# A V table split at column 1024, and every second dense block multiplied in three passes

## The reference

```
def peer_ffn(h, w_query, sub_keys, expert_u, expert_v):      # h: 256 tokens x 2048
    qc = (xc @ w_query).reshape(C, 8, 2, 128)                # 8 heads, two half keys each
    s = einsum('chpd,hpnd->chpn', qc, sub_keys)              # 128 keys per half
    top_s, top_i = top_k(s, 16)
    cand_s = top_s[:, :, 0, :, None] + top_s[:, :, 1, None, :]
    best_s, best_pos = top_k(cand_s over 16 * 16, 16)        # 16 experts of 128 * 128
    g = softmax(best_s)
    u, vv = expert_u[expert_idx], expert_v[expert_idx]       # rows of 2048 floats
    act = gelu(einsum('chkd,cd->chk', u, xc))
    return einsum('chk,chkd->cd', g * act, vv)
```

## Time and profile before

| | us |
|---|---|
| median of three runs | 1690.18 |
| lowest, highest | 1689.35, 1695.68 |
| the profiled execution | 1694.34 |
| its span, first to last instruction | 1692.5 |
| TensorE busy in the span | 1234.9 (73%) |
| VectorE busy | 1298.5 (77%) |
| GpSimd busy | 842.8 (50%) |
| ScalarE busy | 460.9 (27%) |
| moved by DMA | 575.81 MB, 340 GB/s on average |

### The profile page before, as it was taken

How to read it: one execution, slowest core, us unless ns; L and a number is a source line. 1 busy time by engine, 2 the same in 40 slices (tenths; PEclk the granted TensorE clock), 3 DMA queues, 4 the chain that set the end, 5 groups by cost and what they waited for, 6 DMA issues and landing times.

```text
span 1692.5 us, 14464 instructions
## 1 busy us (share of the span) xinstructions
PE 1234.9 (73%) x4812; PEld 839.8 (50%) x4812; DVE 1298.5 (77%) x1802; ACT 460.9 (27%) x1023; POOL 842.8 (50%) x546
## 2 busy tenths in 40 slices
PE   9999999999995554001344544454699999999993
PEld 7888887778984343000122322332365555555551
DVE  5554666466699999999999999999796665666667
ACT  5333443554200100000135565552381000000000
POOL 1000010000174888877888888888565443444444
PEclk9999999999997778555666676666699999999997
DMA  8886546348799999999999999999899999999998
GB/s 237 223 207 196 169 143 213 99 148 278 260 410 415 422 411 396 385 371 362 395 382 407 403 413 387 398 401 422 335 313 380 410 409 411 410 410 409 410 409 347
DMA packets 150230, 575.81 MB, mean 340 GB/s; under 512 B 15586, under 2 KB 28596, under 8 KB 117268
## 3 DMA queue, kind: packets, MB, share of 16 engines
q0 software_dynamic: 74384, 421.30, 62.6%
q1 hardware_dynamic: 75460, 152.82, 26.9%
q10 hardware_dynamic: 320, 0.86, 0.1%
HBM read 572.57 MB, written 2.36 MB: 340 GB/s over the span
## 4 chain that ended last, share of the span: by engine, by line
PE 30%; DVE 28%; DMA 24%; POOL 12%; issue 4%; ACT 2%; DVEq 0%; ACTq 0%; POOLq 0%
DMA v_rows<-in_peer_expert_v,pick_row 21%; DVE big L1549 10%; DVE more_rows L1549 8%; PE ps L1692 6%; PE ps L1694 6%; PE ps L1693 6%; POOL big L691 5%; PE ps L2095 4%; POOL more_rows L691 3%; DVE big L1597 3%; POOL v_rows L671 3%; DMA more_rows<-in_peer_expert_u,pick_row 2%; PE ps L2118 1%; DMA big<-in_peer_expert_u,pick_row 1%; DVE big L1574 1%
## 5 line engine op out<-in xcount | busy, mean ns | idle before, releaser
L671 POOL DMA_INDIRECT v_rows<-in_peer_expert_v,pick_row x256 | 307.8, 1202 | 271.7 <-DVE big L1597 234.9
L1597 DVE SCALAR_TENSOR_TENSOR big<-v_rows,pick_w,big 128x1152 f32<-128x1152 f32 x203 | 287.6, 1417 | 151.7 <-DMA v_rows<-in_peer_expert_v,pick_row 149.7
L2095 PE MATMUL ps<-v_rows,diag 128*128 128x512 f32 (+1 forms) x312 | 182.9, 746 | 269.5 <-DMA v_rows<-in_peer_expert_v,pick_row 169.8
L1549 DVE CUSTOM_DVE_ANT_0 big<-big 128x2048 f32<-128x2048 f32 x150 | 340.1, 2283 | 12.9 <-DMA big<-in_peer_expert_u,pick_row 12.5
L691 POOL DMA_INDIRECT big<-in_peer_expert_u,pick_row x150 | 288.8, 1925 | 65.6 <-issue 43.2
L2095 PEld LDWEIGHTS ps<-v_rows,diag 128*128 128x128 f32 x312 | 83.3, 285 | 368.2 <-issue 194.8
L691 POOL DMA_INDIRECT more_rows<-in_peer_expert_u,pick_row x106 | 222.7, 2101 | 75.3 <-issue 28.3
L1030 DVE TENSOR_TENSOR split_lo<-raw,split_hi 128x1024 fp32r<-128x1024 f32 x119 | 145.8, 1225 | 143.7 <-ACT split_hi L719 118.1
L1549 DVE CUSTOM_DVE_ANT_0 more_rows<-more_rows,big 128x2048 f32<-128x2048 f32 x106 | 240.8, 2284 | 11.0 <-DMA more_rows<-in_peer_expert_u,pick_row 11.0
L2127 PE MATMUL ps<-big,dense 128*128 128x512 f32 (+1 forms) x512 | 213.5, 539 | 0.3 <-DMA big<-in_peer_expert_v 0.3
L2127 PE MATMUL ps<-big 128*128 128x512 f32 (+1 forms) x512 | 213.4, 539 | 0.0
(11 more groups left out here) (281 smaller groups left out, 1495.2 us busy)
## 6 DMA issues: line engine op xcount, KB each, us to landing
big<-in_peer_expert_v SPq DMA_DIRECT2D x128, 448.0 KB, 6.8
raw<-in_w_in SPq DMA_DIRECT2D x88, 512.0 KB, 3.7
raw<-in_w_out SPq DMA_DIRECT2D x32, 512.0 KB, 5.1
big<-in_peer_w_query SPq DMA_DIRECT2D x16, 512.0 KB, 6.5
raw<-in_peer_w_query SPq DMA_DIRECT2D x8, 512.0 KB, 7.6
spare<-in_peer_w_query SPq DMA_DIRECT2D x8, 512.0 KB, 8.3
v_rows<-in_peer_expert_v,pick_row POOLq DMA_INDIRECT x256, 14.2
big<-in_peer_expert_u,pick_row POOLq DMA_INDIRECT x150, 9.1
```

What stands on the lines that cost most here:

```text
L671: pool.indirect_dma_start(v_row(k), None, v_table, bass.IndirectOffsetOnAxis(pick_row[:, k:k + 1], 0)).then_inc(v_gathered[v_place(k)], 16)
L1549: dve.tensor_tensor_reduce(row, row, XN[:, place_of(m // TOPK)[0], :], 1.0, 0.0, ALU.mult, ALU.add, pick_dot[:, m:m + 1]).then_inc(dotted, 1)
L1597: dve.scalar_tensor_tensor(out=v, in0=row, scalar=pick_w[:, k:k + 1], in1=v, op0=ALU.mult, op1=ALU.add).then_inc(added, 1)
L2095: ins = pe.matmul(psf[:, c:c + w], diag[:, j % DIAGS, :], row[:, c:c + w], start=k == 0, stop=j == pe_adds(PICKS) - 1)
```

## The change

- V_ROW goes from 1152 to 1024: a gathered V row set has 128 x 1024 floats, an add on VectorE is 1024 wide, and a dense block has 1024 columns where it had 896.
- The V buffer now holds 5 places in place of 7, since three places of 1024 columns are taken for high parts (`dense_hi`). The places in use beside the dots are 4 where they were 3.
- The U ring is narrow from gather 90 on (108 before), V gathers begin at the dot 99 (115 before), and 40 V picks are added by TensorE beside the dots (36 before). Behind the change-over (still 37 picks) 179 adds are left for VectorE, 183 before.
- Blocks 5, 7, ... 127 (62 of them) are "split blocks". ScalarE copies the block to float32r, and the two 128 x 128 weight blocks as well; VectorE subtracts to get the low parts, in place; TensorE makes three products in the place of one in full float32. The high weights are put where the weights of block a - 4 were.
- VectorE's low parts are put among its adds by `split_after`: those of block a about two blocks ahead of where an even spread of 179 adds over 128 blocks would have it. ScalarE stores the first tile's rows in the midst of its list, behind block 63.

The diff, cut to its core:

```diff
@@ -131,14 +131,14 @@
 RING = 8
 EARLY, EARLY_ROWS = 6, 12
 OLD_HT = 4
-U_WIDE = 108
+U_WIDE = 90
 NARROW = (2, 3, 0, 1, 6, 7)
 WEIGHED = 2
 
-V_ROW = 1152
+V_ROW = 1024
 V_DENSE = D - V_ROW
-V_FROM, V_BESIDE = 112, 36
-V_FIRST_PLACES, V_PLACES = 3, 7
+V_FROM, V_BESIDE = 96, 40
+V_FIRST_PLACES, V_PLACES = 4, 5
 DIAGS = 4
 
 TILE_PICKS = NH * TOPK
@@ -152,6 +152,15 @@
 V_AFTER = V_BESIDE + len(SEAM)
 TURN_BANK = 5
 DENSE_AT = (4 * 512, 6 * 512)
+HI_PLACES, HI_BEHIND = 3, 4
+SPLIT_BLOCKS = [a for a in range(HI_BEHIND, NKEYS) if a % 2]
+SPLIT_AHEAD = 2
+OUT_0_AT = 63
+
+
+def split_after(n):
+
+    return [a for a in SPLIT_BLOCKS if max(0, a - SPLIT_AHEAD) * (PICKS - V_AFTER) // NKEYS == n]
 
 
 def u_place(m):
@@ -384,6 +393,11 @@
         dense_w = (dense0, dense1)
         dense_rows = part(DENSE_PLACES * V_DENSE).rearrange("p (s n) -> p s n", s=DENSE_PLACES)
         assert A_XN <= at_big[0] - DENSE_PLACES * V_DENSE and at_big[0] <= A_X1T
+        at_rows = at_big[0] - DENSE_PLACES * V_DENSE
+        dense_lo = nc.alloc_sbuf_tensor_at("dense_lo", [P, DENSE_PLACES, V_DENSE], F32R, offset=at_sbuf["big"] + 4 * at_rows)
+        split_w = [nc.alloc_sbuf_tensor_at(f"split_w{t}", [P, NKEYS, P], F32R, offset=at_sbuf["big"] + 4 * (A_PROJ if t else A_X1T)) for t in range(TT)]
+        dense_hi = nc.alloc_sbuf_tensor_at("dense_hi", [P, HI_PLACES, V_DENSE], F32R, offset=at_sbuf["ht"])
+        assert HI_PLACES * V_DENSE + V_PLACES * V_ROW <= OLD_HT * D
         hot0 = ring_rest.rearrange("p (s j n) -> p s j n", s=2, j=GROUP_TOKENS)
         hot_at = at_big[0] - (DENSE_PLACES - DENSE_EARLY) * V_DENSE
         hot1 = part(SEAM_HOT * 2 * GROUP_TOKENS * P, hot_at).rearrange("p (i s j n) -> p i s j n", i=SEAM_HOT, s=2, j=GROUP_TOKENS)
@@ -412,6 +426,7 @@
         query_loaded = {n: sem(f"query_loaded_{n}") for n in
                         [k + str(i) for k in ("ahead", "raw", "spare", "ring") for i in range(RAW)] + ["pqt1", "pqt2", "pqt3", "rest0"]}
         query_used = sem("query_used")
+        dense_high, dense_split = sem("dense_high"), sem("dense_split")
 
         def query_name(n):
 
@@ -999,9 +1014,18 @@
                 if ("pe", i) in SEAM_V:
                     pick_diag(SEAM_V["pe", i])
             group_out(1, GROUPS - 1)
-            act.wait_ge(sem("out_ready"), 1)
-            act.wait_ge(added, dve_adds(TILE_PICKS))
-            act.dma_start(out_rows[:, 0, 0:V_ROW], X[:, 0, 0:V_ROW]).then_inc(out_stored, 16)
+            act.wait_ge(group_moved, TT * GROUPS)
+            for r, a in enumerate(SPLIT_BLOCKS):
+                act.wait_ge(dense_loaded[a % DENSE_PLACES], 16 * (a // DENSE_PLACES + 1))
+                act.wait_ge(dense_used, a - HI_BEHIND + 1)
+                act.activation(dense_hi[:, r % HI_PLACES, :], dense_rows[:, a % DENSE_PLACES, :], ACT.Copy).then_inc(dense_high, 1)
+                for t in range(TT):
+                    ins = act.activation(split_w[t][:, a - HI_BEHIND, :], dense_w[t][:, a, :], ACT.Copy)
+                ins.then_inc(dense_high, 1)
+                if a == OUT_0_AT:
+                    act.wait_ge(sem("out_ready"), 1)
+                    act.wait_ge(added, dve_adds(TILE_PICKS))
+                    act.dma_start(out_rows[:, 0, 0:V_ROW], X[:, 0, 0:V_ROW]).then_inc(out_stored, 16)
             act.wait_ge(dense_used, NKEYS)
             v = slice(V_ROW, V_ROW + CHUNK)
             act.activation(X[:, 1, v], ps[:, 6, :], ACT.Copy).then_inc(sem("dense_copied"), 1)
@@ -1654,7 +1678,20 @@
                 hot_pair(i)
                 if ("dve", i) in SEAM_V:
                     v_add(SEAM_V["dve", i])
+            def split_low(a):
+
+                r = SPLIT_BLOCKS.index(a)
+                dve.wait_ge(dense_high, 2 * r + 1)
+                dve.tensor_tensor(dense_lo[:, a % DENSE_PLACES, :], dense_rows[:, a % DENSE_PLACES, :],
+                                  dense_hi[:, r % HI_PLACES, :].bitcast(F32), ALU.subtract).then_inc(dense_split, 1)
+                dve.wait_ge(dense_high, 2 * r + 2)
+                for t in range(TT):
+                    ins = dve.tensor_tensor(split_w[t][:, a, :], dense_w[t][:, a, :], split_w[t][:, a - HI_BEHIND, :].bitcast(F32), ALU.subtract)
+                ins.then_inc(dense_split, 1)
+
             for k in range(V_AFTER, PICKS):
+                for a in split_after(k - V_AFTER):
+                    split_low(a)
                 if k == V_AFTER + V_PLACES:
                     tile_out(dve_adds(k))
                 v_add(k)
@@ -2119,6 +2156,19 @@
 
             def dense(a):
 
+                if a in SPLIT_BLOCKS:
+                    r = SPLIT_BLOCKS.index(a)
+                    pe.wait_ge(dense_split, 2 * r + 2)
+                    hi, low = dense_hi[:, r % HI_PLACES, :], dense_lo[:, a % DENSE_PLACES, :]
+                    for t in range(TT):
+                        w_hi, w_low = split_w[t][:, a - HI_BEHIND, :], split_w[t][:, a, :]
+                        for w, row in ((w_hi, hi), (w_hi, low), (w_low, hi)):
+                            for c in range(0, V_DENSE, CHUNK):
+                                o = DENSE_AT[t] + c
+                                last = a == NKEYS - 1 and w is w_low
+                                ins = pe.matmul(psf[:, o:o + CHUNK], w, row[:, c:c + CHUNK], start=False, stop=last, skip_group_check=True)
+                    ins.then_inc(dense_used, 1)
+                    return
                 pe.wait_ge(dense_loaded[a % DENSE_PLACES], 16 * (a // DENSE_PLACES + 1))
                 row = dense_rows[:, a % DENSE_PLACES, :]
                 for t in range(TT):
```

## The result

The changed kernel took 1717.57 us as the median of four runs (1713.71 to 1718.29), against 1690.36 us before (with one run more than the three of the table above). The ratio is 1.0155 with a 95% interval of 1.0137 to 1.0173: 1.6% slower, where 0.4% faster was forecast, and above the range of 1672 to 1712. It is within half a microsecond of the time that rival 1 gave for a load chain that sets the pace (1718), but that agreement of the numbers is partly luck, as the part on why the prediction was wrong shows.

A forecast was written before the change was run, and what follows sets the result against it. TensorE and DMA were both full in the dense stage, the bound passing to TensorE. TensorE + 10.4, stalls + 6, end - 16.6, U stage - 4, change-over - 2 made 6.2 us less: median 1684.0 us, range 1672 to 1712.

The forecast's parts named there:

- rival 1: Dense stage: the load chain makes TensorE wait for split blocks' low parts; 1718 us at 7.8 us landing; chance 17%.
- The bound: Dense stage: TensorE and DMA both full; bound passes to TensorE at 395.7 us, DMA needing 381.
- TensorE's own term, + 10.4: Dense stage: without waits TensorE ends 10.4 us later; widening costs 55 us, three passes give back 45.
- The stalls: Dense stage: TensorE waits for split blocks' loads, 0.1 us a pair, 6 us in all.
- the bounds 0 and 40: Dense stage: lowest and highest total of TensorE's stalls in us, for load landings from 3.6 to 7.8 us.
- The rule of the Trainium skill: Dense stage: DMA engines alternate between gather and load queues, so loads land as before, 6.8 us; stalls 9 us.
- a point of 6.5: Dense stage: landing time in us up to which nothing stalls; beyond it 30 us for each microsecond.
- The gather ring: Dense stage: five V places are just enough; a gather may take 9.4 us, landing 8 to 10 instead of 14.4.
- Rival 2: Dense stage: five gather places starve VectorE if a gather needs 10.2 us; 29 us more, 1707; chance 11%.
- The U stage and the change-over: Before the dense stage: earlier, smaller V gathers save 4 us in the U stage; narrower adds save 2 in the change-over.
- The end: Behind TensorE's last product: the span ends 9.5 us later instead of 26.1, so 16.6 us come back.
- two of the signs: Wrong if TensorE waits over 20 us for low parts, split products are not near 0.226, or U stage ends later.

The follow-up runs named there:

- The kernel with the fifth place: The changed kernel with a fifth place for dense blocks, taken from one of three places of high row parts: 1693.40 us, ratio 1.0011.
- a sixth place: The changed kernel with six places for gathered V rows instead of five, and two for high row parts instead of three: 1708.45 us, ratio 1.0119.

## Why the prediction was wrong, step by step

**The bound.** Right that TensorE and DMA are both full, that TensorE's own work rises a little, and that the end comes back. TensorE's own term, + 10.4, was right within 1 to 3 us. The kernel without split blocks took 442.6 us from first product to TensorE's end, forecast 441.4. The changed kernel's 426.3 us less 61 x 0.47 of stalls, which come next, are 397.6, against 395.7 and about 1.1 for the last drain. The kernel with the fifth place took 402.9, of which 3 are by its period still waits.

**The stalls: the term that failed.** "I take 6.7, near the 6.6 to 6.8 of the stage ... That is 0.1 us a pair, 6 us in all; between the bounds 0 and 40." The mechanism stood there, with its place and its point of decision; its size was 6.63 - 6.16 = 0.47 us a pair, 29 us by the periods, and 24 by the medians with and without the fifth place. Two things made it so, in about equal parts.

The chain was longer, 10.18 us from the end of block a - 4 to TensorE's start on block a, where I had 9.8. The load is the part that was off: 7.14 us from its issue to ScalarE's start and not 6.7. VectorE's low part then came 1.26 us behind ScalarE and not 1.10, since VectorE was at times late out of an add, and the rest was 0.2 shorter than I had it. I had read the median of the landings, 6.8, where a loop goes by the mean: the odd blocks' was 7.00 already before. The rule of the Trainium skill (DMA: Bandwidth & Descriptors, "SWDGE vs HWDGE vs iDMA"), by which the prediction had a load land as before, is not far off for that, 7.14 against 7.00, but with the 6.8 that was put in it would have made only 9 us of stalls; no view shows packets taking turns.

And the time that TensorE could cover was shorter, 9.22 us and not 9.6. From the start of a split block to the start of the next but one TensorE has 2 x 6.16 = 12.32 us of work, and of this the first block itself takes 3.10 up to the end mark that releases the load, and not 2.72: the marks of the ends are modelled, but by them a block's last product still drains when the next block's first has started. I had put a distance of starts against a chain that begins at an end. With both, (10.18 - 9.22)/2 = 0.48 us a pair, 29 us, where (9.8 - 9.6)/2 = 0.1 was forecast.

**The choice within the bounds.** The rows said that no load in the full stage landed under 6.6 us, against a point of 6.5 with no room for any other hop. With 30 us for each microsecond, a forecast at 0.2 over the point was a forecast on the edge of a slope, and 17% for rival 1 was too little. Rival 1 had the mechanism, but its 1718 was partly luck: it took a landing of 7.8 us and 40 us of stalls, where 29 came, and the rest of the miss came from elsewhere, the U stage above all.

**The gather ring.** Rival 2 was not the cause, but not nothing: a sixth place gave 9 us, mostly through the chain. The forecast of 8 to 10 us for a V row's landing fits the 8.6 of the kernel with six places; of the changed kernel itself the trace has no V landing.

**The U stage and the change-over.** Predicted 4 us saved in the U stage; it costs 3 to 9, and in the two profiles the dots end 5.2 us later (1206.0 against 1200.8). I had priced the narrow ring at 2 us, and counted room at DMA that the narrow ring itself wastes: 280 GB/s from 700 to 720 us, where 410 were moved before. The change-over, from the last dot to the first dense product, took 74.8 us and not 79.2: 4.4 saved, where I took 2 and allowed at most 2.8. Why it gave more was not looked into; with rows of 1024 columns it took between 73 and 80 us in the other profiles.

**The end.** 16.6 predicted, 17.1 measured.

**The whole.** Against the forecast the profiled execution lost 23.4 us in the dense stage and 6.8 before it, and gained 0.5 at the end. TensorE waited for low parts over 20 us and the U stage ended later, two of the signs that the prediction had named for being wrong. Without the chain the change is worth nothing: 11 to 16 us more in the dense stage and some for the U stage against 17 at the end. The gain of the split is spent on the widening.

## What to carry to other kernels

When a step is put between a load and its use, count the loop from the event that releases the load to the use of what it brings, with drains and hops, against the work that the places in between cover; one place more may be worth far more than the step's own time. Take the mean of a wait that stands in such a loop, not its median. Where the loop comes out about as long as its cover (here 9.8 against 9.6), the terms' own uncertainty decides, and the forecast belongs up the slope and not at its foot. Rows that have landed early are a stock: giving up places costs nothing at once, and something when the next stream comes in.

## What the runs showed of the hardware

A dense load of 512 KB beside V rows of 512 KB took hardly longer than one of 448 KB beside V rows of 576 KB: 7.14 us on average from issue to ScalarE's start (changed kernel, split blocks, DMA at 378 GB/s) against 7.00 from issue to landing (before, odd blocks, 410 GB/s). Products of 512 columns in the reduced type cost the same between plain float32 products as back to back: the period with the fifth place is 6.21 us, waits included, against 6.16 from twelve products of 0.2262 us and eight float32 instructions of 0.43. TensorE's waits in the dense stage, up to 2.3 us each, came with no fall of its granted clock, which is 1.00 (2.4 GHz) over the stage.
